# Modulation columns between projection groups, small loads on ScalarE's queue, and norm scale and modulation in one operation

## The reference, cut to what matters

```
ada = silu(c) @ w_ada + b_ada                      # w_ada: 1024 x 6144
sh_m, sc_m, gt_m, sh_f, sc_f, gt_f = split(ada, 6)
h = rms_norm(x, g1) * (1 + sc_m) + sh_m            # feeds the input projection
z = h @ w_in                                       # w_in: 1024 x 6656, split in u, q, k, v, gates
m = mixer(z)                                       # pooling, dilated and window attention
x = x + gt_m * rms_norm(m, g2)
h = rms_norm(x, g3) * (1 + sc_f) + sh_f
x = x + gt_f * rms_norm(moe(h), g4)
```

## Time and profile before

| what | before |
|---|---|
| median of the runs | 1748.67 us |
| profiled execution, time | 1733.79 us |
| its span, first to last instruction | 1732.1 us |
| mean granted TensorE clock | 0.928 of full |
| TensorE busy | 1563.6 us, 90% |
| VectorE, ScalarE, GpSimd busy | 27%, 29%, 15% |
| DMA traffic | 461.29 MB |

### The profile page before, as it was taken

One profiled execution on the slowest core, in us unless ns is written; L12 is line 12 of the kernel. 1 busy time (PEld: TensorE's weight loads), 2 busy tenths in 40 slices (PEclk: granted clock), 3 DMA queues, 4 the chain that ended last, 5 costly groups with the idle time before them and its releaser, 6 DMA issues.

```text
span 1732.1 us, 22957 instructions
## 1 busy us (share of the span) xinstructions
PE 1563.6 (90%) x7181; PEld 881.1 (51%) x7182; DVE 474.7 (27%) x953; ACT 509.6 (29%) x854; POOL 264.9 (15%) x322
## 2 busy tenths in 40 slices
PE   4489999989897999997889879999999999999955
PEld 1057888877764777775345423333333333333311
DVE  2030000145672111111266422222222222212137
ACT  2110000045641000000233234444454444444321
POOL 0030051000300000000111112212122221211153
PEclk7689999966997999998989989999999999999988
DMA  8892379472388936549534299999879998999867
GB/s 289 302 337 26 50 235 331 163 241 64 131 279 257 302 94 203 178 160 329 207 123 169 85 364 393 345 383 411 325 275 342 405 420 341 420 417 422 321 266 249
DMA packets 140516, 461.29 MB, mean 266 GB/s; under 512 B 13401, under 2 KB 78425, under 8 KB 111308
## 3 DMA queue, kind: packets, MB, share of 16 engines
q1 hardware_dynamic: 117853, 331.36, 52.3%
q0 software_dynamic: 22608, 129.18, 21.1%
HBM read 424.80 MB, written 109.28 MB: 308 GB/s over the span
## 4 chain that ended last, share of the span: by engine, by line
PE 79%; DMA 7%; DVE 3%; SPq 3%; POOL 2%; issue 2%; ACT 2%; another core or an unknown queue 1%; ACTq 0%; POOLq 0%; DVEq 0%
PE bank L2107 72%; PE bank L2639 3%; POOL arena L1166 2%; DMA arena<-in_we_down 2%; SPq L783 1%; PE bank L2272 1%; DMA arena<-in_cache_b 1%; PE bank L2661 1%; PE bank L2313 1%; DMA arena<-in_w_in 1%; DMA arena<-in_w_ada 1%; DMA mods<-arena 1%; DMA arena<-in_we_gate 1%; DMA pscale<-in_pool_scale 1%
## 5 line engine op out<-in xcount | busy, mean ns | idle before, releaser
L2107 PE MATMUL bank<-arena 128*64 (+10 forms) x6096 | 1417.0, 513 | 118.4 <-DMA arena<-in_w_ada 26.5
L2107 PEld LDWEIGHTS bank<-arena 128*64 128x64 f32 (+3 forms) x6096 | 748.7, 173 | 680.9 <-issue 467.3
L1184 ACT ACTIVATE arena<-bank 128x512 f32<-128x512 f32 (+6 forms) x152 | 75.1, 505 | 350.5 <-PE bank L2107 219.8
L2026 DVE COPY arena<-bank 128x512 f32<-128x512 f32 x52 | 36.0, 692 | 409.0 <-PE bank L2639 409.0
L1441 ACT ACTIVATE arena<-arena 128x2048 f32 x52 | 99.7, 1918 | 19.5 <-DMA arena<-in_we_gate 15.7
L1128 POOL DMA_INDIRECT arena<-h2rows,icol x54 | 95.6, 1771 | 46.6 <-POOL icol L1124 46.6
L1450 ACT ACTIVATE arena<-arena 128x2048 f32 x52 | 99.3, 1910 | 11.4 <-issue 11.4
L1533 DVE COPY arena<-bank 128x512 f32<-128x512 f32 (+6 forms) x70 | 41.8, 606 | 209.7 <-PE bank L2107 185.8
L1460 ACT ACTIVATE arena<-bank 128x256 f32<-128x256 f32 x52 | 19.9, 383 | 239.5 <-PE bank L2107 239.5
L1323 ACT ACTIVATE arena<-bank 128x288 f32<-128x288 f32 x48 | 19.7, 410 | 233.6 <-PE bank L2107 233.6
L1085 POOL DMA_DIRECT2D out<-in_cache_b x24 | 12.0, 507 | 429.5 <-PE bank L2107 429.5
(11 more groups left out here) (235 smaller groups left out, 732.3 us busy)
## 6 DMA issues: line engine op xcount, KB each, us to landing
arena<-in_we_gate SPq DMA_DIRECT2D x64, 1024.0 KB, 11.2
arena<-in_we_up SPq DMA_DIRECT2D x64, 1024.0 KB, 13.6
arena<-in_we_down SPq DMA_DIRECT2D x64, 1024.0 KB, 11.0
out<-in_cache_b POOLq DMA_DIRECT2D x8, 4080.0 KB, 15.0
yrows<-arena POOLq DMA_DIRECT2D x52, 512.0 KB, 9.2
arena<-in_w_ada SPq DMA_DIRECT2D x12, 2048.0 KB, 16.7
arena<-in_cache_b SPq DMA_DIRECT2D x18, 1024.0 KB, 8.4
arena<-in_w_in SPq DMA_DIRECT2D x7, 2048.0 KB, 15.5
```

What stands on the lines that cost most here:

```text
L1184: act.activation(out, pick(bank), ACT.Copy).then_inc(emptied["A"], 1)
L2026: dve.tensor_copy(xT[:, 512:1024], psb[2][:, :]).then_inc(xt_dve, 1)
L2107: return pe.matmul(out, lhsT, rhs, start=first, stop=last)
```

## The change

Group 0 of the modulation stays at the front. Group 1 is computed in two pairs of pieces, after u and after q3; group 2 after k0 and after k2. VectorE's `ada_group(1)` follows q3, `ada_group(2)` follows k2. The slots are dealt anew: the in loads use slots 0 and 1 (the last one slot 2), ada 4 to 11 use slots 2 and 3. misc, recip, b_ada, gains, one-hot tables, sinks and pool scale are issued by ScalarE's queue, and so are the stores of sh_m and sc_m and the reads of `modb`; the sinks and the pool scale have a semaphore of their own and are issued after the `stab` copies. SiLU is one ScalarE operation instead of Exp, add, reciprocal and multiply. Norm scale and multiplication are one VectorE operation on x. On SyncE's queue the `toep` and `sbias` stores come ahead of in 2 and ada 6 to 11.

```diff
@@ plan()
-    fill(("ada", 1), "D")
+    ring["set"], ring["n"] = list(range(7)), 0
     for t in range(TILES):
         for h in range(2):
             fill(("hT", t, h), "AD"[h])
-        if t == 3:
-            fill(("ada", 2), "D")
...
     for c in range(6):
         for h in range(2):
             fill(("q", c, h), "AD"[h])
+        if c == 3:
+            fill(("ada", 1), "D", 7)
     for g in (0, 1, 2):
         for t in range(TILES):
             fill(("k", g, t), "AD"[t % 2])
+    fill(("ada", 2), "D", 7)
@@ loads()
-    out = [(("ada", g), g % 4) for g in range(12)]
-    out += [(("in", g), g % 4) for g in range(7)]
+    out = [(("ada", g), g) for g in range(4)] + [(("ada", g), 2 + g % 2) for g in range(4, 12)]
+    out += [(("in", g), g % 2 if g < 6 else 2) for g in range(7)]
@@ SyncE
             load(("ada", 2))
             load(("ada", 3))
...
-            for g in range(4, 7):
-                load(("ada", g))
-
-            sp.wait_ge(mods_rows, 1)
...
-            spread(modb, (1, 0), modb_in)
-            for g in range(7, 12):
-                load(("ada", g))
+            load(("in", 0))
+            load(("in", 1))
+            load(("ada", 4))
+            load(("ada", 5))
+            sp.wait_ge(fills_done, INDEX[("hT", 0, 1)] + 1)
             sp.dma_start(staterow[0:NB * PSTATE, :], state_pool[0].rearrange("b t c -> (b t) c")).then_inc(state_in, 16)
-            for g in range(4):
-                load(("in", g))
...
                 sp.dma_start(sbias[h0:h1].rearrange("h t k -> h (t k)"),
                              stab[h0:h1, n * NT * NK:(n + 1) * NT * NK]).then_inc(tables_out, 16)
+            load(("in", 2))
+            load(("ada", 6))
+            load(("ada", 7))
+            load(("in", 3))
+            load(("ada", 8))
+            load(("ada", 9))
+            load(("in", 4))
+            load(("ada", 10))
+            load(("ada", 11))
             sp.wait_ge(mods_rows, 2)
...
-            for g in range(4, 7):
+            for g in range(5, 7):
                 load(("in", g))
@@ ScalarE
+            act.dma_start(misc[:], const[:, 3 * P:4 * P]).then_inc(consts_in, 16)
...
             act.wait_ge(crow_in, 32)
-            act.activation(crow[0:9, D:2 * D], crow[0:9, 0:D], ACT.Exp, scale=-1.0).then_inc(c_exp, 1)
+            act.activation(crow[0:9, D:2 * D], crow[0:9, 0:D], ACT.Silu).then_inc(c_silu, 1)
+            for j in range(4):
+                act.dma_start(ada[32 * j:32 * j + 32, :, :],
...
             act.activation(stat[:, 0, :], stat[:, 0, :], ACT.Sqrt).then_inc(root_ready, 1)
+            act.wait_ge(mods_rows, 1)
+            for j in range(4):
+                act.dma_start(mods[:, j // 2, 512 * (j % 2):512 * (j % 2) + 512], ada[32 * j:32 * j + 9, 0, :]
+                              ).then_inc(mods_out, 16)
+            act.wait_ge(mods_out, 16 * 4)
+            for n, q in enumerate((1, 0)):
+                act.dma_start(modb[:, 2 * n, :], mods[0:1, q, :].broadcast_to([P, D])).then_inc(modb_in, 16)
...
-                    act.activation(hbuf[0:r, t % 2, :], xall[0:r, t, :], ACT.Copy,
-                                   scale=stat[0:r, 0, t:t + 1]).then_inc(xn_ready, 1)
@@ VectorE
-            link(dve.tensor_scalar(ce, ce, 1.0, None, ALU.add))
-            link(dve.reciprocal(ce, ce))
-            dve.tensor_tensor(crow[0:9, 0:D], crow[0:9, 0:D], ce, ALU.mult).then_inc(c_silu, 1)
...
-            dve.wait_ge(gains_in, 16 * 8)
+            dve.wait_ge(gains_in, 16 * 4)
...
-                dve.wait_ge(xn_ready, t + 1)
-                dve.tensor_tensor(hbuf[0:r, t % 2, :], hbuf[0:r, t % 2, :], modb[0:r, s, :],
-                                  ALU.mult).then_inc(hA_ready, 1)
+                if t >= 2:
+                    wait_fill(dve, ("hT", t - 2, 1))
+                dve.scalar_tensor_tensor(hbuf[0:r, t % 2, :], xall[0:r, t, :], stat[0:r, 0, t:t + 1], modb[0:r, s, :],
+                                         ALU.mult, ALU.mult).then_inc(hA_ready, 1)
...
+                if c == 3:
+                    ada_group(1)
+                    ada_row(2, 0.0, False)
...
+            ada_group(2)
+            ada_row(4, 1.0, False)
+            ada_row(5, 0.0, True)
@@ TensorE
-            for kk in range(4):
-                ada_piece(1, kk)
             for t in range(TILES):
                 pe.wait_ge(h_ready, t + 1)
                 transposed_rows("hT", t, hbuf[:, t % 2, :])
-                if t < 4:
-                    ada_piece(2, t)
...
             for c in range(4):
                 by_channel(("u", c), w, c * P)
+            ada_piece(1, 0)
+            ada_piece(1, 1)
             w = wait_load(pe, ("in", 1))
             for c in range(4):
                 by_channel(("q", c), w, c * P)
+            ada_piece(1, 2)
+            ada_piece(1, 3)
             w = wait_load(pe, ("in", 2))
...
                 if g == 1:
+                    ada_piece(2, 0)
+                    ada_piece(2, 1)
                     w = wait_load(pe, ("in", 3))
...
+            ada_piece(2, 2)
+            ada_piece(2, 3)
```

More of the change, by code:

```diff
@@ L437, in build @@
         ada = at(A_VTM, 3, 512)
-        gains = at(A_VTM + 6 * D, 3, 512)
+        gains = at(A_VTM + 3 * 512, 3, 512)
         crow = at(A_VTM + 10 * D, 2 * D)
@@ L1184, in empty @@
                 act.activation(out, pick(bank), ACT.Copy).then_inc(emptied["A"], 1)
+            act.dma_start(misc[:], const[:, 3 * P:4 * P]).then_inc(consts_in, 16)
+            act.dma_start(recip[:], const[:, 4 * P:4 * P + 64].rearrange("p (g n) -> p g n", g=4)
+                          ).then_inc(consts_in, 16)
             act.wait_ge(crow_in, 32)
-            act.activation(crow[0:9, D:2 * D], crow[0:9, 0:D], ACT.Exp, scale=-1.0).then_inc(c_exp, 1)
+            act.activation(crow[0:9, D:2 * D], crow[0:9, 0:D], ACT.Silu).then_inc(c_silu, 1)
+            for j in range(4):
+                act.dma_start(ada[32 * j:32 * j + 32, :, :],
+                              bass.AP(tensor=b_ada.tensor, offset=b_ada.offset + 512 * j,
+                                      ap=[[0, 32], [2048, 3], [1, 512]])).then_inc(badd_in, 16)
+            for (a, half), g in (((0, 1), g_pre_mix), ((1, 0), g_post_mix), ((2, 0), g_pre_ffn), ((2, 1), g_post_ffn)):
+                act.dma_start(gains[64 * half:64 * half + 64, a, :],
+                              bass.AP(tensor=g.tensor, offset=g.offset, ap=[[512, 2], [0, 32], [1, 512]])
+                              ).then_inc(gains_in, 16)
+            act.dma_start(oh_top[0:BINS, :], onehot_top).then_inc(onehots_in, 16)
+            act.dma_start(oh_smp[0:BINS, :], onehot_smp).then_inc(onehots_in, 16)
+            act.dma_start(relT[0:32, :], rel_bias).then_inc(onehots_in, 16)
             act.wait_ge(x_in, 32)
@@ L1200, in _ @@
             act.activation(stat[:, 0, :], stat[:, 0, :], ACT.Sqrt).then_inc(root_ready, 1)
+            act.wait_ge(mods_rows, 1)
[5 more added lines that the diff above has]
+                act.dma_start(modb[:, 2 * n, :], mods[0:1, q, :].broadcast_to([P, D])).then_inc(modb_in, 16)
+                act.dma_start(modb[0:NS, 2 * n + 1, :],
+                              bass.AP(tensor=mods.tensor, offset=(6 + q) * D, ap=[[6 * D, NB], [0, NT], [1, D]])
+                              ).then_inc(modb_in, 16)
             for n in range(7):
@@ L1203, in _ @@
                 empty(("stab", n), stab[0:20, 480 * n:480 * n + w], lambda b: b[0:20, 0:w])
[L1206 to L1211, removed]
-                    act.activation(hbuf[0:r, t % 2, :], xall[0:r, t, :], ACT.Copy,
-                                   scale=stat[0:r, 0, t:t + 1]).then_inc(xn_ready, 1)
[L1214 to L1217, removed]
-                          lambda b: b[:, 0:4 * r].rearrange("p (k n) -> p k n", k=4))
-            act.wait_ge(mods_rows, 2)
+            act.dma_start(sinkb[:], sinks.broadcast_to([P, 8])).then_inc(sinks_in, 16)
+            for b in range(2):
+                act.dma_start(sinkr[64 * b:64 * b + 64, :],
+                              bass.AP(tensor=sinks.tensor, offset=sinks.offset, ap=[[1, 8], [0, 8], [1, 1]])
+                              ).then_inc(sinks_in, 16)
+            act.dma_start(pscale[:], pool_scale[0].rearrange("(m p) -> p m", p=P),
+                          allow_slow_non_contiguous=True).then_inc(sinks_in, 16)
+            for t in range(TILES):
+                r = parts(t)
+                empty(("hT", t, 0), hT[:, 0:4, toks(t)],
+                      lambda b: b[:, 0:4 * r].rearrange("p (k n) -> p k n", k=4))
             for c in range(4):
@@ L1575, in _ @@
                 empty(("gtab", n), gtab[0:20, n * GW:(n + 1) * GW], lambda b: b[0:20, 0:GW])
-            ada_group(1)
             for t in range(TILES):
@@ L1610, in _ @@
                 empty(("q", c, 1), qT[:, c, 288:TOK], lambda b: b[:, 0:288])
+                if c == 3:
+                    ada_group(1)
+                    ada_row(2, 0.0, False)
+                    dve.wait_ge(sinks_in, 16 * 4)
```

(3 more changed lines are left out.)

15 lines of the change are left out of this document (2 added, 13 removed).

## The result

The changed kernel takes 1802.68 us, median of 4 runs (1798.25 to 1811.34), against 1748.74 us (1744.22 to 1750.66, 4 runs) of the kernel before. The ratio is 1.0319, 95% interval 1.0279 to 1.0359: 53.9 us slower, where 30 were forecast, and 2.7 us above the upper end of the range.

The account below looks back on a forecast made before the run. TensorE's unbroken projection was taken as the bound. Its start 36.5 us earlier, less 15.4 for moved pieces and 51 for a new wait, gave an end 29.8 us later: 1778.7 us, range 1752 to 1800.

Parts of the forecast that it names:

- The new wait: TensorE after q3 waits for ada 6, whose load SyncE issues only after the table stores; costs 51 us.
- the 112 taken from the earlier trace: SyncE's time from first toep issue until its queue is free: 112 us, bounds 104 to 120.
- The moved pieces: Eight modulation pieces moved from the front into the projection, where TensorE doesn't wait: full cost, 15.4 us.
- T0: First toep issue, waiting until the first tile of h is transposed: put at 62.6 us.
- The gains and b_ada must have landed by 39.8: Front: these small loads were assumed present when group 0's bias is added, at 39.8 us.
- The bounds of T0, 55 and 80: Range for the first toep issue, from fast or slow landings of modulation stores and reads.
- The third rival: Modulation stores and reads land as slowly on ScalarE's queue as before; first toep issue at 80, kernel 1796 us; chance 0.13.
- The sign given for a start of the projection at 90 or later: Sign of a wrong forecast: such a start would put the fault in the landing of stores and modb reads.
- The fourth rival: Small loads stand long in ScalarE's issue, squares and bias late; first toep issue moves up to 10 us, inside the range.
- the loads behind the tables: Three 2.1 MB loads after SyncE's table stores: 15.9 us at 396 GB/s, plus 2 us until landing.
- The share of engines: Table stores called slow because four or eight heads engage four or eight of sixteen DMA engines (0.23, 0.46).
- The first two rivals: Table stores out in under 60 us, 21 to 22 us faster, 0.09; or held 75 to 90, within 0.5%, 0.08.

Follow-up runs that it names:

- e6: Changed kernel with the 20 toep rows stored once in DRAM and copied 128 times from DRAM to DRAM: 1757.81 us, ratio 1.0055 to the kernel before.
- e8: Kernel before with only the two fused operations (SiLU; norm scale and modulation): 1749.92 us, ratio 1.0010.
- e10: Kernel before with only the small loads moved to ScalarE's queue, sinks and pool scale no longer waited for by the modulation: 1753.95 us, ratio 1.0056.
- e3: Changed kernel with each gain load of 64 partitions split into two of 32: 1795.24 us, ratio 1.0264 to the kernel before.
- e5: Changed kernel with SyncE waiting for the modb reads before issuing in 0, in 1, ada 4 and ada 5: 1789.05 us, ratio 1.0251 to the kernel before.
- e2: Changed kernel with each head's toep row stored by its own DMA, 20 instead of 4: 1816.66 us, ratio 1.0410 to the kernel before.
- e13: Changed kernel with table stores started when their rows are ready, not after the first transposed tile, and the pooling state loaded earlier: 1762.89 us, ratio 1.0131.

## Why the prediction was wrong

**Right: what bounds the kernel, and the sign.** The end of the projection carries the time, in all thirteen kernels. The new wait stands where the prediction put it, at ada 6 after q3, for the reason it gave: SyncE stands in the table stores, 111.1 us against the 112 taken from the earlier trace rows. That this fits to 1 us is in part luck. In the kernel before, in 0 to 3 were still under way when SyncE came to the stores (two windows below: 387 and 257 GB/s, and 31 from 125 us on), so some 12 of its 112 us were not the stores. In the changed kernel the engines moved 43 GB/s from 88.7 us on, so by the same reading about 100 us were to be expected, and it took 111. The prediction's lower bound, 104, allowed for some of this.

```profile
115.00:120.00 5.00, 5.00 (x22) 3.94 (x21) 0.25 (x1) 0.41 (x1) 0.00 (x0) 1.00 1.05 387
120.00:125.00 5.00, 5.00 (x22) 3.91 (x21) 0.41 (x3) 0.41 (x1) 2.51 (x5) 1.00 0.70 257
```

The pause was 49.55 us and 1.72 behind it, against 51. The moved pieces cost their full length: 253.57 us of unbroken projection in e6 against 238.54 are 15.0 us, against 15.4. The fused operations were worth nothing (e8).

**Wrong: the size of T0.** It was put at 62.6 and measured at 88.7, 26.1 us more, and the end moved with it. Step by step:

| term of T0 | put at | measured | more |
|---|---|---|---|
| bias added | 39.8 | 57.4 | 17.6 |
| stores of the rows, from the end of their issue to landing | 3.5 | 5.4 | 1.9 |
| modb reads, from the end of their issue to landing | 8 | 13.5 | 5.5 |
| row, issues, first tile, state issue | 11.3 | 12.4 | 1.1 |

The largest term fell at one sentence: "The gains and b_ada must have landed by 39.8". I took the gains off the path with the pool scale. In the kernel before, a wait for eight DMAs in one semaphore had been put down to the last of them, and the row could not say when the gains had come; I read it as if they had long been there. SyncE's own rows of that trace could have warned me: it stood some 20 us in these issues, and the last gain's ended only at 38.35.

```profile
17.85 11.61 SPq L783 DMA_DIRECT2D arena<-in_g_post_mix  x1
29.50 3.57 SPq L783 DMA_DIRECT2D arena<-in_g_pre_ffn  x1
33.12 5.23 SPq L783 DMA_DIRECT2D arena<-in_g_post_ffn  x1
```

They land late in the changed kernel, and in e10 as well. e3 shows that 11.3 of the 17.6 us are theirs. The other 6.3 are ada 3's: its piece began at 43.12 and not at 36.1, so the 2 us (0 to 4) added for the small loads beside the big ones were 9. The landings of stores and reads were too short by 7.4 us together; e5, with SyncE's big loads held back, has 1.2 and 8.3 us for them, so the price of those loads beside them was put too low.

The bounds of T0, 55 and 80, were too narrow for the same reason: they let the landings of stores and reads vary and held the gains fixed. The third rival, which raised T0 to 80 by two slow landings, gave 1796 and came nearest, but its mechanism is not the main one: landings made 7.4 of the 26.1 us. The sign given for a start of the projection at 90 or later (it was 101.7) pointed at these landings too, and so at the smaller part. The fourth rival had the right place: the small loads stand long in ScalarE's issue and the bias comes late. But it bounded the shift at 10 us and was counted as inside the range; the bias alone was 17.6 us late.

**Smaller: the loads behind the tables.** From SyncE's last sbias store to ada 7's piece there were 24.8 us, put at 18. With the rest of the projection it makes 3.8 us: T0 + 319.6, put at T0 + 315.8. 29.8 + 26.1 + 3.8 = 59.7, the measured shift of the end of the projection (59.8). The median moved by 53.9; part of the 6 us between them is the spread of the runs, and which of the later stages gave something back is not settled.

**Wrong but without effect: why the stores are slow.** The share of engines was right as a reading and wrong as a cause (e2, e6). The 112 us of the rows didn't need the cause. But a remedy built on it, e2, made the kernel slower.

**The first two rivals** fell: SyncE was held, and for the full time. That a stand of 82 us would have been the point from which the kernel is slower was reckoned with T0 at 62.6. With T0 at 88.7 there is no such point: the front wins 8.3 us and the moved pieces cost 15, so the kernel is slower by some 7 us without any pause, as e6 shows.

## What to carry to other kernels

When work is moved behind a transfer in one issuing engine's queue, price the transfer by how long that engine stands in it, and look for the first load behind it that someone needs; moving the compute off the front wins nothing if that load's issue hangs on the same front. A wait on one semaphore for several DMAs hides all but the last of them: before taking the last one off the path, ask when each of the others lands. And look at small loads by their form: moved to a second queue as they were, they landed later here; in pieces of 32 rows the same loads turned a loss of 0.6% into a gain of 0.4%.

## What the runs showed of the hardware

- Copying an SBUF row to DRAM 128 times ran at 26 to 34 GB/s with all reads from four neighbouring partitions or fewer, whether 0.23 or 0.87 of the DMA engines were busy (39 GB/s on average in e13, unexplained), at 55 with eight, and at 264 GB/s when the row was read from DRAM instead.
- SyncE and ScalarE stood in DMA issues while what they had issued before was still slow on its way: SyncE 111 us in eight table stores, ScalarE 18.20 us in a gain load of 128 KB and 13.53 us in the one-hot load behind it. SyncE was through e6's fast copy of the same table in 0.64 us, and GpSimd issued the four slow stores in 4.6 us.
- How long SyncE stood in the same stores was 111 us with their start at 88.7 and 89.6 us with their start at 65.0; the cause is open.
